# The turns of the activations move behind the second half of the up and gate products

## What is computed

```
def expert_block(args):
    tok, e = args
    xb = h_ext[tok]
    act = jax.nn.silu(xb @ w_gate[e]) * (xb @ w_up[e])
    return act @ w_down[e]
yb = lax.map(expert_block, (tok_pad.reshape(n_blocks, MOE_BLOCK), blk_e))
yb = yb.reshape(P, D) * w_pad[:, None].astype(h.dtype)
return jnp.zeros((T + 1, D), h.dtype).at[tok_pad].add(yb)[:T]
```

## Time and profile before

| | |
|---|---|
| median of three runs | 1204.73 us |
| profiled execution: span from first to last instruction | 1207.1 us |
| mean granted TensorE clock (of 2.4 GHz) | 0.978 |
| busy: PE, DVE, ACT, POOL | 94%, 39%, 30%, 24% |
| the chain that ended last: PE, DMA, ACT | 87%, 6%, 2% |
| of that, up and gate (L1422), down (L1441) | 27%, 13% |
| stage of the experts | about 565 to 1181 us of the span |

### The profile page before, as it was taken

One profiled execution on the slowest core, in us unless ns is written; L12 is line 12 of the kernel. 1 busy time (PEld: TensorE's weight loads), 2 busy tenths in 40 slices (PEclk: granted clock), 3 DMA queues, 4 the chain that ended last, 5 costly groups with the idle time before them and its releaser, 6 DMA issues.

```text
span 1207.1 us, 16330 instructions
## 1 busy us (share of the span) xinstructions
PE 1133.4 (94%) x5082; PEld 546.7 (45%) x5083; DVE 475.5 (39%) x1035; ACT 362.7 (30%) x732; POOL 290.6 (24%) x226
## 2 busy tenths in 40 slices
PE   6999999998999999997899999988999999999981
PEld 5898444454456666655333333322333333333320
DVE  3560019953556656345323232222223232322334
ACT  3221100025655556311232222312332323223232
POOL 0110199930000000111121222211221212222133
PEclk9999999999999999998999999989999999999995
DMA  8127211012411111186873999999699999999344
GB/s 259 26 35 143 40 36 35 1 70 75 159 69 53 53 53 53 53 347 263 336 270 79 390 394 374 413 411 412 238 406 375 397 405 372 408 360 408 108 156 168
DMA packets 86271, 262.60 MB, mean 218 GB/s; under 512 B 31973, under 2 KB 49132, under 8 KB 61630
## 3 DMA queue, kind: packets, MB, share of 16 engines
q1 hardware_dynamic: 68868, 243.43, 52.5%
q0 software_dynamic: 11632, 17.44, 6.3%
q10 hardware_dynamic: 5706, 0.92, 0.4%
HBM read 245.38 MB, written 27.00 MB: 226 GB/s over the span
## 4 chain that ended last, share of the span: by engine, by line
PE 87%; DMA 6%; ACT 2%; issue 1%; DVE 1%; SPq 1%; POOL 1%; ACTq 0%; DVEq 0%; POOLq 0%
PE psum L1422 27%; PE psum L1117 13%; PE psum L1441 13%; PE psum L1315 9%; PE psum L1114 4%; PE psum L1260 3%; DMA W<-in_w_gate 3%; PE psum L1280 3%; PE psum L1408 3%; PE psum L1112 3%; PE psum L1429 2%; PE psum L1271 2%; DMA W<-x_rows 1%; PE psum L1344 1%; DMA W<-in_x 1%
## 5 line engine op out<-in xcount | busy, mean ns | idle before, releaser
L1422 PE MATMUL psum<-W,RD 128*64 (+1 forms) x800 | 368.2, 604 | 15.3 <-DVE RD L1945 14.4
L1423 PE MATMUL psum<-W,RD 128*64 128x512 f32 x800 | 368.3, 604 | 0.0
L1422 PEld LDWEIGHTS psum<-W,RD 128*64 128x64 f32 x800 | 106.6, 139 | 225.7 <-issue 219.8
L1927 DVE TENSOR_TENSOR RD<-psum,RD 128x256 f32<-128x256 f32 x50 | 21.2, 424 | 417.0 <-ACT RD L1031 417.0
L1441 PE MATMUL psum<-W,RD 128*64 (+1 forms) x400 | 184.6, 605 | 0.7 <-ACT RD L1035 0.7
L1442 PE MATMUL psum<-RD 128*64 128x512 f32 x400 | 184.6, 605 | 0.0
L731 POOL DMA_INDIRECT x_rows<-RD,tabi x48 | 78.0, 1625 | 442.7 <-ACT RD L1042 433.0
L1117 PE MATMUL psum<-W 128*128 128x512 f32 x384 | 166.9, 593 | 0.4 <-ACT W L849 0.4
L1315 PE MATMUL psum<-W,RD 128*128 128x512 f32 x256 | 118.2, 594 | 1.6 <-ACT RD L925 1.1
L1117 PEld LDWEIGHTS psum<-W 128*128 128x128 f32 x384 | 72.5, 191 | 88.0 <-issue 87.2
L1423 PEld LDWEIGHTS psum<-W,RD 128*64 128x64 f32 x800 | 106.7, 139 | 0.0
(11 more groups left out here) (340 smaller groups left out, 1272.8 us busy)
## 6 DMA issues: line engine op xcount, KB each, us to landing
W<-in_w_up SPq DMA_DIRECT2D x32, 2048.0 KB, 13.3
W<-in_w_gate SPq DMA_DIRECT2D x32, 2048.0 KB, 18.3
W<-in_w_down SPq DMA_DIRECT2D x32, 2048.0 KB, 20.5
W<-in_x SPq DMA_DIRECT2D x16, 512.0 KB, 4.8
W<-in_w_in SPq DMA_DIRECT2D x5, 1024.0 KB, 12.2
W<-in_w_in SPq DMA_DIRECT2D x16, 256.0 KB, 4.3
x_rows<-W SPq DMA_DIRECT2D x8, 512.0 KB, 2.9
h_rows<-RD SPq DMA_DIRECT2D x8, 512.0 KB, 3.6
```

The lines of the kernel that those rows point to most:

```text
L1422: pe.matmul(bank(2)[0:HALF].rearrange("p (g n) -> p g n", g=2), x, near, start=k == 0, stop=k == KD - 1)
L1423: ins = pe.matmul(bank(2)[HALF:P], x, upgate1[:, k].rearrange("p g n -> p (g n)"), start=k == 0, stop=k == KD - 1)
```

## The change

The two lines of `aT(b)` in TensorE's `step` move behind the second half of the products, directly ahead of `xT`.

```
                 up_gate(base, 0)
+                pe.wait_ge(ex_cu, full)
+                up_gate(base, 1).then_inc(ex_u, 1)
                 if not first:
                     aT(b)
-                pe.wait_ge(ex_cu, full)
-                up_gate(base, 1).then_inc(ex_u, 1)
                 xT((q + 1) % AHEAD, got)
                 if not first:
                     down(bank(4 + (1 - q % 2)), prev, b, None if isinstance(freed, int) and freed <= 0 else freed)
```

## The result

The changed kernel takes 1254.03 us (median of 4 runs, 1252.01 to 1257.58) against 1206.23 for the kernel before (4 runs): the ratio is 1.0389, 95% interval 1.0367 to 1.0410. It is 3.9% slower. The forecast was 1251 us in a range of 1230 to 1276. The profiled execution has a span of 1251.8 us, against 1207.1 before.

The account below looks back on a forecast made before the run. The expert stage was taken as bound by TensorE, at 11.71 us a step. 47 steps of 13.03 us plus 2 for weights gave 614.4 against 568.05, +46.4 us, so 1251.1 us, range 1230 to 1276.

Parts of the forecast that it names:

- What TensorE saves: Between the product halves: 0.58 us removed, 0.25 added in the joint turn group, so 0.33 us a step shorter without new waits.
- the prediction's first wait: On TensorE, down waits 0.23 us for the evicted activations; TensorE's own step is still 0.1 us shorter than before.
- Down's wait for the eviction: Ahead of down on TensorE: down starts at M+1.69, a wait of 0.23 us, bounds 0 and 0.33.
- M: Start of the last product pair of a step's second half on TensorE; later times in the step count from it.
- ScalarE's queue: Table reads wait behind the late eviction and delay silu; TensorE then waits 1.4 us at every step's start.
- A: Time ScalarE's queue needs for the table reads, counted from the eviction's start: 2.1 to 3.2 us, mean 2.5.
- The new chain from M: Eviction, reads, silu, product, copy, scaling, next step's first pair: 4.08 + A, put at M+6.58; step 13.03 us.
- Weights: Weight loads: the old stretch of waiting (17.6 us with its half-clock pairs) is nearly all absorbed; 2 us of waiting left.
- The sum: 47 steps of 13.03 us give 612.4, plus 2 for weights: 614.4 us against 568.05, +46.4 us.
- The rival that the reads run ahead: ScalarE's queue passes the waiting eviction, silu comes right behind it; 4.6 us faster, 1200 us; chance 0.09.
- no difference: Rival: the eviction's wait eats the whole 0.33 us saving and the reads run ahead; 1204 us; chance 0.03.
- The clock rival: TensorE's idle lowers its granted clock once a step, 1.7 us each, 80 us in all: 1330 us; chance 0.05.

Follow-up runs that it names:

- e1: Changed kernel with ScalarE's eviction of the turned activations moved behind the next block's four table reads: 1202.63 us, ratio 0.9971 to the kernel before.
- e5: e1 with the row turns ahead of the activation turns in the joint group: 1220.06 us, ratio 1.0113 to the kernel before.
- e4: Changed kernel with two more table reads, values unused, behind the four that follow the eviction: 1322.04 us, ratio 1.0959 to the kernel before.
- e6: e1 with the eviction split between VectorE and ScalarE from two accumulator banks, down's wait for it put last: 1204.54 us, ratio 0.9974 to the kernel before.

## Why the prediction was right

*What TensorE saves* held. The halves are joined, and e1 shows the result by itself: 11.58 us a step where nothing else is late, against the 11.61 that the prediction's first wait leaves (0.1 less than 11.71).

*Down's wait for the eviction* held: M+1.66 and in some steps 1.80, against 1.69, with a saving of 0.33 of which 0.1 is left. e5 shows the cover at work from the other side.

*ScalarE's queue* was the step that decided, and it is shown by four doses: none, two, four and six reads behind the eviction give steps of 11.58, 11.79, 13.02 and 14.10 us. The mean from eviction to silu over steps 1 to 47 is 2.50 us, where A + 0.08 = 2.58 was used; A reached 2.8 at most, where the old trace has values up to 3.2. The new chain from M was put at 6.58 and is 6.54 in the median.

*Weights*: absorbed as forecast. 2 us were to be left over, and it was one wait of 1.98 before the copy. Behind it came one fall of the clock to the lower level, 1.7 us, that the sum did not have. The fall at the start of step 1 was no part of the weight stretch. The prediction counted its 1.7 us among the 17.6 that would be absorbed, and they stayed.

*The sum*: 47 steps were to take 614.4 us and took 615.28. Such closeness is partly luck. A was 0.08 too long and the way from a step's first pair to M 0.03 too short (6.48 against 6.45), together 2.4 us too much in 47 steps. The two falls of the clock (at 577 and 843 us, 3.4 us) made up for it. The step from span to time was wrong: the prediction took 2.4 us off, but the profiled run of the changed kernel took 1253.65 us with a span of 1251.8. The span was put 1.7 us too high and the time 2.9 too low.

*The rival that the reads run ahead* fell in the changed kernel: the first read starts at 703.6, behind the eviction's start at 703.25, after 5.88 us in which ScalarE idled. But its price was right for the kernel in which they do stand ahead: 4.6 us were given, e1 gained 4.1 in the steps and 0.29% of the time. With it fell *no difference*, which needed it too. *The clock rival* fell at 0.9 to 1.7 us of idle a step. In e4 it came true in part.

What stays open: why the clock fell in some of e4's steps and not in others with the same idle time, and what e6 would take without the hold at its end.

## What to carry to other kernels

When a signal is moved later, look at what stands behind the instruction that waits for it on its engine, register reads included: they need no data from it and are still held. A hole that hides work in one order is gone in the other, so move the work ahead of the wait together with the signal. And a chain beside the busy engine costs nothing until it is longer than that engine's own work (here 5.14 us from M in e1). From there on it costs what it is longer.

## What the runs showed of the hardware

- A queue instruction behind an activation whose semaphore is open does not run: the table reads of step 10 stood still through ScalarE's 5.88 us of idle ahead of the eviction. A read takes 0.28 us, and 0.61 with its register work in that step; e4's two more reads add 1.07 us, 0.53 each. Where the semaphore was met and only the engine was busy, the queue ran on: once in the kernel before, the first read starts at 847.7 us and the eviction ahead of it, behind a weight copy, at 849.19.
- From the end of an eviction to the product that waited for it 0.21 us go by in e1's step 6 (646.21 to 646.42), 0.25 in e6 and 0.35 in e1's step 4 (622.78 to 623.13). In step 4 TensorE's queue (PEldq in the view) has an ALU_OP between the semaphore instruction and the address work (first rows). In step 6 the wait ends with the eviction and the address work follows (last rows). Down starts at M+1.80 and M+1.66. In e6, where the wait for the evictions stands last, down starts at M+1.59 to M+1.64 in all but one of the loop's steps. That the ALU_OP makes the difference was not tested by itself:

```profile
L1438 PEldq EVENT_SEMAPHORE  x1: 51/51/51, 622.8 to 622.8; - x1
L1440 PEldq ALU_OP  x1: 32/32/32, 622.9 to 622.9; - x1
L1443 PEldq FUSED_REGOPS  x4: 46/46/46, 623.0 to 623.5; - x4
...
L1440 PEldq EVENT_SEMAPHORE  x1: 3827/3827/3827, 642.4 to 642.4; - x1
L1443 PEldq FUSED_REGOPS  x2: 46/46/46, 646.3 to 646.4; - x2
```

- In e4 most steps up to 1049 us had 2.4 to 2.8 us of idle, and from 635 to 1049 us the granted clock fell ten times, 44 to 58 us apart from start to start, at 1.7 us each. After that most steps had 2.0 to 2.1 us of idle, and it fell once more, at 1188 us. In the changed kernel, with 0.9 to 1.7 us a step, it fell within the 47 steps only behind the 3.62 and 3.29 us of idle at 577 and 842 us.
